# Last gate chunks six at a time in block order with the third block halved, and sums of squares in two bfloat16 halves

## What is computed

```python
h = h + concat([y_a, y_b, y_c]) @ w_out
hn = rmsnorm(h, norm_ffn)
up = hn @ w_up
upc, new_ffn = causal_dwconv(st_ffn, up, ffn_conv)
h = h + (silu(upc[..., :D_FF]) * upc[..., D_FF:]) @ w_down
gate = sigmoid(rmsnorm(h, norm_ple) @ ple_gate)
h = h + (p_i @ ple_proj) * gate
...
y = rmsnorm(h, norm_final)      # x * rsqrt(mean(x * x) + eps) * gain, over the 2048 features
```

## Time and profile before

| | us |
|---|---|
| median of three runs | 3097.07 |
| the three runs | 3071.39, 3097.07, 3230.68 |
| time of the profiled execution | 3073.51 |
| its span, first to last instruction, on the slowest core (core 6) | 3072.0 |
| spans of the eight cores | 3063.6 to 3072.0 |
| PE busy, PE idle on that core | 3012.6, about 59 |

### The profile page before, as it was taken

The page is one execution under the profiler, slowest core; times in us unless marked ns, Lnnn a source line. Parts: engine busy times, 40 slices in busy tenths (PEclk is TensorE's granted clock), DMA queues, the critical chain, the costliest instruction groups (busy, mean ns, idle before and its releaser), DMA issues.

```text
span 3072.0 us, 57946 instructions; the slowest of 8 cores (3063.6 to 3072.0 us)
## 1 busy us (share of the span) xinstructions
PE 3012.6 (98%) x20766; PEld 1946.8 (63%) x20766; DVE 1711.6 (56%) x3458; ACT 863.8 (28%) x1691; POOL 457.7 (15%) x672
## 2 busy tenths in 40 slices
PE   6999999999999999999999999999999999999996
PEld 3566666666666666666666666666666666666664
DVE  3465437555565555646545753565555555665656
ACT  4132123212121213315541412231213131331465
POOL 0000131100000000005310002301000000001532
PEclk9999999999999999999999999999999999999998
DMA  8645636644444444454456356346454444444433
GB/s 195 137 74 85 105 54 97 96 75 75 76 75 75 75 76 75 71 83 66 66 98 128 61 93 110 63 83 102 69 88 74 81 76 78 70 88 77 71 63 124
DMA packets 122552, 263.22 MB, mean 86 GB/s; under 512 B 36256, under 2 KB 64416, under 8 KB 122272
## 3 DMA queue, kind: packets, MB, share of 16 engines
q0 software_dynamic: 74112, 213.48, 42.9%
q1 hardware_dynamic: 43264, 37.97, 4.8%
q10 hardware_dynamic: 4896, 8.07, 1.0%
HBM read 449.11 MB, written 15.97 MB: 151 GB/s over the span
## 4 chain that ended last, share of the span: by engine, by line
PE 95%; DMA 2%; DVE 1%; ACT 1%; issue 0%; SPq 0%; POOL 0%; DVEq 0%; POOLq 0%; ACTq 0%
PE ps L131 95%; DMA wb<-w_up 1%; DMA h<-xT 1%; DMA wb<-w_in 1%; DMA U<-hf 0%; SPq L131 0%; DVE U L131 0%; DVE h L131 0%; ACT L131 0%; ACT rstd L131 0%; DMA U<-hc 0%; DVE xa L131 0%; ACT U L131 0%; POOL U L131 0%; ACT xb L131 0%
## 5 line engine op out<-in xcount | busy, mean ns | idle before, releaser
L131 PE MATMUL ps<-xa,wb 128*128 128x364 bf16 (+6 forms) x9456 | 1458.3, 315 | 30.2 <-DMA wb<-w_in 20.4
L131 PE MATMUL ps<-xb,wb 128*128 128x366 bf16 (+7 forms) x9456 | 1433.3, 312 | 1.5 <-DMA wb<-w_up 1.0
L131 PEld LDWEIGHTS ps<-xa,wb 128*128 128x128 bf16 x9456 | 921.9, 98 | 547.9 <-issue 45.8
L131 PEld LDWEIGHTS ps<-xb,wb 128*128 128x128 bf16 x9456 | 921.9, 98 | 495.0 <-issue 6.5
L131 DVE SCALAR_TENSOR_TENSOR U<-ps,cstt,U 128x348 f32<-128x348 f32 (+3 forms) x1056 | 607.5, 578 | 428.9 <-ACT U L131 372.4
L131 ACT ACTIVATE U<-ps,cstt 128x364 f32<-128x364 f32 (+2 forms) x528 | 291.1, 553 | 1178.2 <-PE ps L131 1114.6
L131 DVE TENSOR_TENSOR h<-ps,h 128x364 f32<-128x364 f32 (+4 forms) x672 | 349.0, 523 | 411.8 <-PE ps L131 410.2
L131 ACT ACTIVATE U<-h 128x344 bf16<-128x344 f32 (+9 forms) x336 | 162.2, 495 | 404.4 <-DVE h L131 388.0
L131 POOL TENSOR_TENSOR U<-U 128x364 f32<-128x364 f32 (+4 forms) x252 | 218.2, 868 | 338.7 <-ACT U L131 337.3
L131 ACT ACTIVATE U<-U 128x364 f32<-128x364 f32 (+3 forms) x402 | 197.4, 491 | 240.9 <-DVE U L131 176.7
L131 DVE TENSOR_TENSOR U<-ps,rstd 128x364 f32<-128x364 f32 (+10 forms) x300 | 153.5, 525 | 196.0 <-PE ps L131 183.8
(11 more groups left out here) (62 smaller groups left out, 817.8 us busy)
## 6 DMA issues: line engine op xcount, KB each, us to landing
wb<-w_up POOLq DMA_DIRECT2D x176, 512.0 KB, 5.7
wb<-w_in POOLq DMA_DIRECT2D x68, 512.0 KB, 7.3
wb<-w_down POOLq DMA_DIRECT2D x64, 448.0 KB, 5.8
wb<-w_out POOLq DMA_DIRECT2D x32, 512.0 KB, 6.4
wb<-w_down POOLq DMA_DIRECT2D x32, 512.0 KB, 5.4
wb<-ple_gate POOLq DMA_DIRECT2D x32, 512.0 KB, 5.2
h<-xT SPq DMA_DIRECT2D x8, 728.0 KB, 31.4
yT<-h SPq DMA_DIRECT2D x6, 728.0 KB, 3.5
```

Source lines behind the costliest of these rows:

```text
L131: ins = getattr(e, name)(*a, **kw)
```

## The change

Three things change together.

1. `TAIL` goes from 4 to 6 in both layers: chunks 0 to 9 one at a time, and chunks 10 to 15 block by block. In the last layer the third block is halved there (182 and 182 columns), so that the order is six steps of block 0, six of block 1, six of each half.
2. In all six `Stats` places the float32 accumulator is no longer an operand of TensorE. With the last chunk that goes to the accumulator, POOL writes the sum rounded to bfloat16 (`hx`), the float32 sum, and their difference in bfloat16 (`lx`). TensorE multiplies `hx`, `lx` and the squares of the last `nd` chunks with the bfloat16 ones. `nd` is 1, in the last layer's gate 2, and 4 for the last half block. `NSQ` goes from 3 to 6. There are two pairs of `hx` and `lx` tiles, taken in turn.
3. In the last layer's gate, `lag` brings the sum of a block forward by one tick, that of the first half block by two. The final norm takes chunks 4, 8, 12 and 0 in this order, and the group of chunk 0 runs on POOL. The final gain of the half blocks is on POOL. One piece of `bg` is drained after each step of blocks 0 and 1 and after every other one of the halves. A one-column Ln on ACT stands after the last sigmoid.

The diff, cut to its core:

```diff
-NSQ = 3
+NSQ = 6
-TAIL = 4
+TAIL = 6
-SQZ_O = 5920
+SQZ_O = 5264
...
+            def pieces(blk):
+                return [(*blk(b), b, ([0], [1], [2, 3])[b]) for b in range(3)]
...
                     self.sq = many("sq", o, WB, NSQ, BF16)
-                    self.acc = many("sa", o + NSQ * WB // 2, WB, blk.n)
+                    self.acc = many("sa", o + NSQ * WB // 2, WB, 3)
+                    self.hl = many("hl", o + NSQ * WB // 2 + 3 * WB, WB, 4, BF16)
...
-                def add(self, m, b):
+                def add(self, m, pc, nd=1, lag=3):
...
+                    if m < KC - nd:
+                        if m == KC - nd - 1:
+                            (hx, hxB), (lx, lxB) = self.hl[self.nh % 4], self.hl[self.nh % 4 + 1]
+                            self.nh += 2
+                            self.parts[lo] = [(hx[:, 0:n], hxB), (lx[:, 0:n], lxB)]
+                            S.op("pool", (lambda e: e.tensor_tensor(out=hx[:, 0:n], in0=av, in1=sv, op=ALU.add)), reads=[sqb, saB], writes=[hxB])
+                        S.op("pool", (lambda e: e.tensor_tensor(out=av, in0=av, in1=sv, op=ALU.add)), reads=[sqb], writes=[saB])
+                        if m == KC - nd - 1:
+                            S.op("pool", (lambda e: e.tensor_tensor(out=lx[:, 0:n], in0=av, in1=hx[:, 0:n], op=ALU.subtract)), reads=[saB, hxB], writes=[lxB])
+                        return
+                    self.parts[lo].append((sv, sqb))
                     if m < KC - 1:
-                        S.op("pool", (lambda e: e.tensor_tensor(out=sa[:, 0:n], in0=sa[:, 0:n], in1=sq[:, 0:n], op=ALU.add)), reads=[sqb], writes=[saB])
                         return
+                    parts = self.parts.pop(lo)
                     def go():
                         slot = bank()
-                        S.op("pe", (lambda e: e.matmul(ps_t[:, slot, 0:n], lhsT=onesf_t[:], rhs=sa[:, 0:n], start=True, stop=False)), ...)
-                        mm(slot, n, 1, (lambda k: ones_t[:]), (lambda k: sq[:, 0:n]), [onesB, sqb], first=False)
+                        mm(slot, n, len(parts), (lambda k: ones_t[:]), (lambda k: parts[k][0]), [onesB] + [o for _, o in parts])
...
-                    pend.append((st["tick"], go))
+                    pend.append((st["tick"] + lag - 3, go))
...
+                whole = pieces(eb)
+                halves = whole[0:2] + [(CUT2, CUT3, 2, [2]), (CUT3, W, 2, [3])]
...
-                    for k in range(0, KC, 4):
+                    for i, k in enumerate((4, 8, 12, 0)):
+                        eng = "pool" if k == 0 else "dve"
+                        q = i % 2 if end_ else 0
...
                     if last:
-                        S.op("act", (lambda e: e.activation(out=h1(m, lo, hi), in_=h1(m, lo, hi), func=AF.Identity, scale=cs("nfin", m))), ...)
+                        emb["stats"].add(m, pc, 4 if lo == CUT3 else 2, 1 if (lo, hi) == (CUT2, CUT3) else 2)
+                        g = cs("nfin", m)
+                        if lo >= CUT2 and hi - lo < WB - 12:
+                            S.op("pool", (lambda e: e.tensor_scalar(out=h1(m, lo, hi), in0=h1(m, lo, hi), scalar1=g, scalar2=None, op0=ALU.mult)), ...)
+                        else:
+                            S.op("act", (lambda e: e.activation(out=h1(m, lo, hi), in_=h1(m, lo, hi), func=AF.Identity, scale=g)), ...)
...
+                    if last and hi == W and m == KC - 1:
+                        S.op("act", (lambda e: e.activation(out=scr_t[:], in_=ones_t[:, 0:1], func=AF.Ln)), reads=[onesB], writes=[scrB])
                     emb_rest()
-                    drain(2)
+                    drain(1 if last and (lo < CUT2 or m % 2) else 0)
...
-                    for b in range(eb.n):
+                    pcs = halves if last and len(ms) > 1 else whole
+                    for pc in pcs:
```

More of the change, by code:

```diff
@@ L260, in program @@
             RA, RB, RU = Region(), Region(), Region()
-            cstB, gainB, onesB, nsB = Buf("cst"), Buf("gain"), Buf("ones"), Buf("ns")
+            cstB, gainB, onesB, nsB, scrB = Buf("cst"), Buf("gain"), Buf("ones"), Buf("ns"), Buf("scr")
             psB = [Buf(f"ps{i}") for i in range(8)]
@@ L342, in tick, with hb @@
                     pend.pop(0)[1]()
+            def pieces(blk):
+                return [(*blk(b), b, ([0], [1], [2, 3])[b]) for b in range(3)]
+            def hb(m, pc):
+                return [hB[m][i] for i in pc[3]]
             class Stats:
@@ L357, in add @@
                     sa, saB = self.acc[b]
+                    av = sa[:, o:o + n]
                     if m == 0:
-                        S.op("act", (lambda e: e.activation(out=sa[:, 0:n], in_=h1(m, lo, hi), func=AF.Square)), reads=of(hB[m], b, self.blk.n), writes=[saB])
+                        S.op("act", (lambda e: e.activation(out=av, in_=h1(m, lo, hi), func=AF.Square)), reads=hb(m, pc), writes=[saB])
                         return
                     sq, sqb = self.sq[self.n % NSQ]
+                    sv = sq[:, 0:n]
@@ L935, in program, with final_norm, go @@
                 emb = {"n": 0, "prev": None, "stats": None}
-                def final_norm(b):
-                    lo, hi = eb(b)
-                    for k in range(0, KC, 4):
[L940 to L945, removed]
+                whole = pieces(eb)
+                halves = whole[0:2] + [(CUT2, CUT3, 2, [2]), (CUT3, W, 2, [3])]
+                def final_norm(pc):
+                    lo, hi, b, idx = pc
+                    end_ = hi == W
+                    for i, k in enumerate((4, 8, 12, 0)):
+                        eng = "pool" if k == 0 else "dve"
+                        q = i % 2 if end_ else 0
+                        def go(k=k, eng=eng, q=q):
+                            rd = [o for i in range(k, k + 4) for o in hb(i, pc)]
+                            S.op(eng, (lambda e: e.tensor_tensor(out=hv(h_t, k, 4, lo, hi), in0=hv(h_t, k, 4, lo, hi), in1=rstd_t[:, lo:hi].unsqueeze(1).broadcast_to([128, 4, hi - lo]),
+                                                                 op=ALU.mult)), reads=[rsB[i] for i in idx], writes=rd)
+                            S.dma(("sp", "act")[q], (lambda e: e.dma_start(out=hv(yT, k, 4, lo, hi), in_=hv(h_t, k, 4, lo, hi))), f"s_y{q}", reads=rd)
                         bg.append((b, go))
@@ L973, in emb_step @@
                     f, fresh[b] = fresh[b], False
-                    sg_ = proj(wv[:, 0], X_t, lo, hi, wbuf, [[xold[k][min(b, 2)]] for k in range(KC)], f)
+                    sg_ = proj(wv[:, 0], X_t, lo, hi, wbuf, [[xold[k][b]] for k in range(KC)], f)
                     sp_ = bank()
```

54 lines of the change are left out of this document (27 added, 27 removed).

## The result

The changed kernel takes 3121.44 us at the median of its 16 runs, 3095.22 at the lowest; the kernel before, on the same chips, 3097.23 and 3071.24. The ratio is 1.0099 with an interval of 1.0067 to 1.0132: about 1% slower. That is within 2% of the time before, but outside the range of the prediction, 3078 us with 3065 to 3100. In many executions of the changed kernel, and by their times of the kernel before on that chip, one pair of cores has a lower granted clock before 460 us and comes about 26 us late (in the profile after cores 4 and 5: core 4 has 0.92 there, core 6 has 1.00), so stages are read from the other cores, and the ratios leave out executions with a whole die at a lower clock.

The account below looks back on a forecast made before the run. PE's matmuls bound the kernel up to about 3047 us, then the last block's rstd and final norm. 3073.5 + 6.2 (tail) - 1.3 (sums outside the tail) = 3078.4, so 3078 us, range 3065 to 3100.

Parts of the forecast that it names:

- last term of the tail: After the last norm piece: 4.9 us before; the last DMA has half the bytes, so 1 us off.
- ledger of the shared path: Last gate and norm: DVE 16.5, POOL 21.1, open chains 7.0, handovers 0.5: 45.1 us; last norm piece +7.2.
- bound of 0.51: Upper bound in us for a POOL gain of 182 columns, from two-input operations; 0.33 taken, lower bound 0.13.
- open chains: Last gate: ACT's rstd chains of block 1 and the first half are not covered by steps: 7.0 us.
- PE's last projection: Sign of being right: about 10 us later than before, 15 us from there to the end where it was 26.
- Sums outside the tail: Five sums of squares places: -2.7 + 1.4 = -1.3 us, between -4.4 and +0.3; each down place loses 0.7.
- 2.7 us to be won in the other three places: Output projections and first gate: cheaper bfloat16 matmuls win 3 x 0.89 us; the extra POOL additions cost nothing.
- `TAIL` 6 in the first layer: Layer change: ring slots held until block 2, next layer's first weights load late; 0 taken, upper bound 3.6 us.
- ring rival: Second layer's first weights come late, as those of w_up do: 3078 + 3.6 = 3082 us; chance 0.08.
- Narrow matmuls: Half steps: 182 columns take 78 ns a matmul, 1.41 us a step; if bound by 98 ns loads, 4.3 us more.
- clock rival: Second half: after PE's waits, steps at 1.2 GHz last 2.8 instead of 1.4 us: 3078 + 3.5 = 3082; chance 0.12.
- shorter tail: Rival: POOL's work slips into DVE's gaps in the last gate; about 3067 us, 6 faster; chance 0.24.

Follow-up runs that it names:

- e8: Changed kernel with its output written in whole rows and the half blocks' gains moved from POOL to ACT: 3087.24 us (one run).
- e7: Changed kernel with whole output rows, third block not halved, gains on ACT and all final norm groups on DVE: 3075.68 us (lowest of 2).
- e10: e7 with a third pair of hx and lx for the two down projections only: 3072.16 us (one run).
- e9: e7 with the float32 sums of squares of before in all places but the last gate: 3071.92 us, ratio 0.9993 to the kernel before.
- e5: Kernel before with the new bfloat16 sums of squares alone (TAIL 4, whole blocks, old final norm): 3084.92 us, ratio 1.0033.
- e12: e7 with the float32 sums of squares of before in all places: 3069.82 us, ratio 0.9989 to the kernel before.
- e3: Changed kernel writing 176 of each half's 182 columns, rows of 704 bytes placed at multiples of 64 bytes: 3090.75 us (one run).
- e4: Changed kernel writing 176 of each half's 182 columns, 704-byte rows left where the change has them: 3101.15 us (one run).
- e2: Kernel before with each of the third block's four output DMAs split in two of 182 columns: 3089.23 us.

## Why the prediction was wrong

The median of 3121.44 us stands 43 above the forecast for two reasons. The forecast was put on an execution of 3073.5, and the median before is 3097.23: 24 us of level, not of the change. And the change cost 24.2 us between the medians (24.0 between the lowest, 26.4 in the stages) where the sum had 4.9. The range was also too narrow by its own logic: its end of 3100 lets the level reach 3097 but leaves no room for the 5 us of the forecast on top.

**The step that failed** is the last term of the tail: "the last DMA has half the bytes now, for which I take 1 us off". It was worth +13.0 us instead of -1, half of the 26.4 us between the table's columns. Rows of before did carry a warning that was not used: block 0's DMAs, rows of 1248 bytes, took 54 ns a packet, 23 bytes a nanosecond, where whole runs took 5824 bytes in 225 ns, 26. That row would have given about 32 ns for 728 bytes, close to the 35 that the first half rows took, so a loss of a factor of two to three could not be read from it; but that the DMA changed from one run to four rows a partition was in the diff, and no rival priced it.

**The ledger of the shared path** came out in its sum (45.3 us against 45.1, the tail +8.0 against +7.2 for its last norm piece) and not in its parts. A gain that met no DVE operation took 0.74 to 0.85 us, above the bound of 0.51 taken from two-input additions, of which one of 182 columns took 0.53; twelve of them should have lengthened the path by 12 x 0.5 = 6 us over the 0.33 each of the ledger, and taking them off POOL (e8) gave 0.5. The norm groups on POOL cost 3.5 us. The largest part, 6.3 us, is the halving itself (e7), which the prediction had only as "open chains" (7.0 us) within the ledger. So the mechanism of the ledger, one path that every operation adds to, was not what set the stretch in all its parts, and that its sum came within 0.2 us is in part luck: a gain was too cheap in it, and more of POOL's work was taken to lie on the path than edits give back. POOL was busy for 33.7 us of the stretch (3030 to 3075.4 us, its waits for the path included), not 21.1. PE's last projection came 16 us later than before and 33 us ahead of the end, where 10 and 15 were forecast.

**Sums outside the tail**: -1.3 predicted, +5.4 measured, outside the bounds of -4.4 to +0.3. The mechanism was the predicted one, block 0's sums behind block 2's last POOL operation; e10, which takes away the shared pair, gives back 4.4 us. The size was not. PE waits 2.4 to 2.5 us at each down place, where 1.6 were worked out (2920.1 - 2918.50). POOL's nine operations were sized right: they took from 2909.69 to 2914.51 + 3.85 = 2918.36, 8.7 us for 8.6. But PE started 0.25 us after them, and it came to the place 6.5 us after POOL's first of the nine, not 7.0 as in the earlier trace rows. The fall of the clock behind the wait, an estimated 1.7 us a place, was not in the sum at all. It falls on the sums or on the projection behind them: the nine matmuls took 2.69 us and the next projection 3.14 here, 1.67 and 4.17 in e5, and 0.62 for the last three and 2.63 in e10, where the wait was 1.66. The 2.7 us to be won in the other three places don't show (e9 and e10), nor could they in so few profiles.

**`TAIL` 6 in the first layer** cost nothing, as predicted: PE's waits for `w_in` are 19.9 us in all after and 20.4 before. The ring rival is out. **Narrow matmuls** came at 78 ns as taken: 1.41 us for the step from 3046.75, so the weight load of 98 ns did not bound them. The rule of the Trainium skill that was weighed there (TensorE: Matmul & The Clock Gate, LDWEIGHTS) gives 107 ns a load. The spacing measured is below that, so by this trace the rule's figure does not set it.

**The clock rival** was right as a mechanism: the stalls of 4.56 and 3.51 us, both within the halves, were each followed by a step of 2.63 us. Its price of 3.5 us was not needed in the sum, so the longer steps probably lay beside the shared path's work; no run took them away alone. **The shorter tail** is out for the change as made, but the tail is 4.5 us shorter in e12, without the halves and POOL's new work. What speaks for the shared path as told in the Trainium skill (SBUF — State Buffer, Who interferes with whom) is the pair of rows at 3035.06: a DVE operation with both inputs in SBUF held for the whole length of POOL's.

## What to carry to other kernels

When a block is split, look at what its output DMA becomes in HBM: with eight cores writing at once, four rows of 728 bytes at odd places ran at a third of the rate of one run, rows of 704 on multiples of 64 bytes did not, and the last DMAs have nothing to hide under. Halving the last block shortens its last piece but adds a whole chain from square to rstd, and halves what lies over each; weigh it against the steps that cover the chain. Before moving a sum to a cheaper number format, count what the conversion adds on the engine that was already last, and check that rotating buffers are as many as the blocks recorded before the first is read.

## What the hardware showed beyond that

- HBM writes by rows of 704 bytes took 34 ns a packet throughout when start and length were multiples of 64 bytes (e3). With most starts off that grid (e4) they took 34 ns at first on the cores that began first, and later up to 121 ns, as medians of stretches of 2 us.
- The slowness reached packets that were not off the grid: whole runs of 5824 bytes took about 400 ns in e2, core 6, 3060 to 3064 us, against 225 in the kernel before.
- POOL's operation with one input and a scalar for each partition took 0.74 to 0.85 us alone for 182 columns, longer than its addition of two inputs of the same width, 0.50 to 0.53.
- After PE's wait of 2.45 us at the last down place, in a stretch otherwise full, part of the next matmuls ran at 1.2 GHz: those of 364 columns stood 0.30 us apart, and 0.15 at full clock. After the wait of 1.66 us in e10 none did.
